# The first tiles of a decoder trunk's input projection in another order, and the norm's weight row spread with 128 rows of weights

## The reference

```
def rms_norm(x, g):
    xf = x.astype(jnp.float32)
    y = xf * lax.rsqrt(jnp.mean(xf * xf, axis=-1, keepdims=True) + EPS)
    return (y * g.astype(jnp.float32)).astype(x.dtype)

def trunk_layer(x, p, k_past, v_past, ...):
    h = rms_norm(x, g_pre_mix)
    cb, cc, ch, q, k, v, ga, gb = jnp.split(h @ w_in, IN_SPLITS, axis=-1)
    ...   # gated short convolution, stick-breaking attention, projections
    x = x + rms_norm(merged @ w_o, g_post_mix)
    ...   # up-projection, convolution, gelu gate, down-projection, input embedding
```

## Time and profile before

| | |
|---|---|
| median of three runs | 1679.24 us (1679.14 to 1679.53) |
| the profiled execution | 1680.04 us |
| its span, first to last instruction | 1678.3 us |
| TensorE busy | 1667.5 us, 99% of the span |
| VectorE, ScalarE, GpSimd busy | 1101.4, 794.6, 321.0 us |
| moved by transfers | 170.64 MB, 102 GB/s in the mean |

### The profile page before, as it was taken

The page is one execution under the profiler, slowest core; times in us unless marked ns, Lnnn a source line. Parts: engine busy times, 40 slices in busy tenths (PEclk is TensorE's granted clock), DMA queues, the critical chain, the costliest instruction groups (busy, mean ns, idle before and its releaser), DMA issues.

```text
span 1678.3 us, 27174 instructions
## 1 busy us (share of the span) xinstructions
PE 1667.5 (99%) x9101; PEld 1462.9 (87%) x9101; DVE 1101.4 (66%) x1606; ACT 794.6 (47%) x1391; POOL 321.0 (19%) x268
## 2 busy tenths in 40 slices
PE   9999999999999999999999999999999999999998
PEld 8999998999999999988888888888888878888886
DVE  7365246325533646547688888888888688776576
ACT  7345344444534453125454444444444444465675
POOL 2000000000000000002346666666664000000000
PEclk9999999999999999999999999999999999999999
DMA  5312221132123114443132222222222852245333
GB/s 182 97 55 74 80 77 55 57 99 68 60 67 92 53 63 149 151 169 116 68 97 80 79 79 79 79 72 72 79 79 97 293 191 80 90 150 186 112 123 118
DMA packets 176598, 170.64 MB, mean 102 GB/s; under 512 B 16207, under 2 KB 144555, under 8 KB 176492
## 3 DMA queue, kind: packets, MB, share of 16 engines
q1 hardware_dynamic: 165546, 164.41, 30.5%
q10 hardware_dynamic: 10946, 4.91, 1.0%
HBM read 129.66 MB, written 39.62 MB: 101 GB/s over the span
## 4 chain that ended last, share of the span: by engine, by line
PE 94%; DVE 3%; DMA 1%; issue 1%; SPq 1%; ACT 0%; DVEq 0%; POOL 0%; POOLq 0%; ACTq 0%
PE pair L3152 11%; PE pair L2840 9%; PE pair L2842 9%; PE pair L2841 9%; PE pair L3212 8%; PE pair L3214 8%; PE pair L3213 8%; PE pair L2794 6%; PE pair L3368 3%; PE pair L3370 3%; PE pair L3369 3%; PE pair L3221 3%; PE pair L3021 2%; PE pair L2771 2%; PE pair L2769 2%; PE pair L2770 2%
## 5 line engine op out<-in xcount | busy, mean ns | idle before, releaser
L2840 PE MATMUL pair<-xh,wh 128*128 128x384 f32 (+1 forms) x952 | 324.4, 341 | 0.0
L2842 PE MATMUL pair<-xh,wl 128*128 128x384 f32 (+1 forms) x952 | 311.3, 327 | 0.0
L2841 PE MATMUL pair<-xl,wh 128*128 128x384 f32 (+1 forms) x952 | 310.8, 326 | 0.0
L2840 PEld LDWEIGHTS pair<-xh,wh 128*128 128x128 f32 x952 | 179.3, 188 | 5.4 <-issue 4.0
L2841 PEld LDWEIGHTS pair<-xl,wh 128*128 128x128 f32 x952 | 179.4, 188 | 0.0
L2842 PEld LDWEIGHTS pair<-xh,wl 128*128 128x128 f32 x952 | 178.8, 188 | 0.0
L1074 POOL TENSOR_TENSOR srow<-hn,hn 128x512 f32<-128x512 f32 x8 | 12.0, 1506 | 791.1 <-DVE hn L2322 790.8
L3368 PE MATMUL pair<-woph,foph 128*128 128x512 f32 x308 | 120.9, 393 | 0.1
L3370 PE MATMUL pair<-woph,fopl 128*128 128x512 f32 x308 | 120.0, 390 | 0.0
L3369 PE MATMUL pair<-wopl,foph 128*128 128x512 f32 x308 | 120.0, 390 | 0.0
L1408 ACT ACTIVATE keep<-pair,bias 128x512 f32<-128x512 f32 (+4 forms) x100 | 58.2, 582 | 115.6 <-DVE pair L2175 71.5
(11 more groups left out here) (417 smaller groups left out, 4289.5 us busy)
## 6 DMA issues: line engine op xcount, KB each, us to landing
rawp<-in_w_up SPq DMA_DIRECT2D x88, 256.0 KB, 3.8
raw<-in_w_in SPq DMA_DIRECT2D x80, 256.0 KB, 3.2
wd<-in_w_down SPq DMA_DIRECT2D x55, 256.0 KB, 3.0
f_spill<-cv SPq DMA_DIRECT2D x22, 552.0 KB, 2.8
f<-f_spill SPq DMA_DIRECT2D x44, 256.0 KB, 5.6
gat<-gate_spill SPq DMA_DIRECT2D x16, 544.0 KB, 4.5
x_spill<-x SPq DMA_DIRECT2D x16, 512.0 KB, 3.0
gate_spill<-stg SPq DMA_DIRECT2D x32, 192.0 KB, 1.9
```

What stands on the lines that cost most here:

```text
L2840: t_.matmul(b, h, xhi, start=(k == 0), stop=False, skip_group_check=True)
L2841: t_.matmul(b, h, xlo, start=False, stop=False, skip_group_check=True)
L2842: ins = t_.matmul(b, l, xhi, start=False, stop=(k == KD - 1), skip_group_check=True)
```

## The change

It has five parts.

- `grow` becomes 128 rows of which row 0 is the weight row that counts: `ones` is 128 x 128 with ones in row 0 and zeros elsewhere. Rows 0 to 31 of `grow` are loaded (a broadcast of the same row, 128 KB), rows 32 to 63 are zeroed by GpSimd, rows 64 to 127 by VectorE. The result is the same row on all partitions.
- The fillers go from 34 to 14: six before the row products, eight behind them.
- The products of the first tiles are reordered: block 0's high products come first, before its low part and the low weights are waited for, turn 2 comes earlier among them, and in the other two units the products with the part that comes latest stand last.
- ScalarE makes block 0's high part ahead of block 2's square.
- The low weights of job 1 are made by VectorE in place of GpSimd.

```diff
-WARM = (8, 4, 11, 5, 6)
+WARM = (8, 6)
...
-        grow, ones = a.take("grow", [1, D]), a.take("ones", [1, P])
+        grow, ones = a.take("grow", [P, D]), a.take("ones", [P, P])
...
+            pool.wait_ge(g_const, 1)
+            g.memset(grow[32:64, :], 0.0).then_inc(g_grow, 1)
+            pool.wait_ge(g_grow, 1)
             then(g.memset(far[:, :], 0.0))
...
-            for j in range(2):
-                pool.wait_ge(a_hi, j + 1)
-                minus(wl[j][:, :], raw[j][:, :], f(wh[j][:, :])).then_inc(g_wlo, 1)
+            pool.wait_ge(a_hi, 1)
+            minus(wl[0][:, :], raw[0][:, :], f(wh[0][:, :])).then_inc(g_wlo, 1)
...
-            act.dma_start(grow[:, :], inp["g_pre_mix"]).then_inc(row_in, 16)
+            act.dma_start(grow[0:32, :], inp["g_pre_mix"].rearrange("l d -> (l d)").partition_broadcast(32)).then_inc(row_in, 16)
...
             whi()
+            x0_high(0)
             x0_square(2)
-            x0_high(0)
...
-            v.memset(ones[:, :], 1.0).then_inc(d_ones, 1)
+            then(v.memset(ones[:, :], 0.0))
+            v.memset(ones[0:1, :], 1.0).then_inc(d_ones, 1)
+            v.memset(grow[64:P, :], 0.0).then_inc(d_ones, 1)
...
                     x0_scaled(3, 1, 4)
-                    wlo_by_pool()
+                    wlo()
...
                 def by_blocks():
                     b = open_unit(0, 0)
...
+                    o, cols = b[:, 0:P], slice(0, P)
+                    pe.wait_ge(a_hi, 1)
+                    pe.wait_ge(a_x0h, 2)
+                    for k in range(KD):
+                        t_.matmul(o, tall(0, k)[0], xh[:, k, cols], ...)
+                    begin_job()
+                    pe.wait_ge(d_x0l, 2)
+                    for k in range(KD):
+                        if k == 3:
+                            x0_turn(2)
+                        h, l = tall(0, k)
+                        t_.matmul(o, h, xl[:, k, cols], ...)
+                        t_.matmul(o, l, xh[:, k, cols], ...)
+                    o, cols = b[:, P:3 * P], slice(P, 3 * P)
+                    for k in range(KD):
+                        if k % KH == 0:
+                            pe.wait_ge(a_x0h, 5 + k // KH)
+                        h, l = tall(0, k)
+                        t_.matmul(o, h, xh[:, k, cols], ...)
+                        t_.matmul(o, l, xh[:, k, cols], ...)
+                    pe.wait_ge(d_x0l, 6)
+                    for k in range(KD):
+                        ins = t_.matmul(o, tall(0, k)[0], xl[:, k, cols], ...)
+                    ins.then_inc(p_unit, 1)
...
                 if first:
-                    idle(4)
-                    pe.wait_ge(d_ones, 1)
+                    idle(1)
+                    pe.wait_ge(d_ones, 2)
+                    pe.wait_ge(g_grow, 1)
                     pe.wait_ge(row_in, 16)
...
                     idle(0)
                     x0_turn(0)
-                    idle(1)
                     x0_turn(1)
-                    idle(2)
-                    begin_job()
                     by_blocks()
-                    begin_job()
-                    in_tile(1, 0, {1: [(x0_turn, 3)], 3: [(x0_turn, 4)], 5: [(x0_turn, 5)]})
-                    pe.wait_ge(d_x0l, 12)
-                    conv_rows()
-                    in_tile(0, 1, {6: [(x0_turn, 6)]})
+                    weight_low_last(1, 0, {1: 3, 7: 4, KD + 1: 5})
+                    block_low_last(0, 1, {6: 6})
                     past(0)
```

More of the change, by code:

```diff
@@ L520, in build @@
         a_sum, d_sum = sem("a_sum"), sem("g_wlo_d_sum")
-        g_wlo, SUM0 = d_sum, 2
+        g_grow, SUM0 = d_sum, 2
+        g_wlo, WLO0 = d_sum, 1
         d_lo = sem("d_lo")
@@ L1977, in wlo_by_pool @@
             def wlo_by_pool():
-                dve.wait_ge(g_wlo, job.step())
+                dve.wait_ge(g_wlo, WLO0 + job.step())
                 dve.sem_inc(d_lo, 1)
@@ L2854, in idle @@
                     for _ in range(WARM[i]):
-                        turned(banks[1 if i in (2, 3) else 7][:, 0:P], ident[:, :])
+                        turned(banks[7][:, 0:P], ident[:, :])
                 def by_blocks():
                     b = open_unit(0, 0)
[L2860 to L2871, removed]
+                    o, cols = b[:, 0:P], slice(0, P)
@@ new lines, in by_blocks @@
+                    pe.wait_ge(a_hi, 1)
+                    pe.wait_ge(a_x0h, 2)
+                    for k in range(KD):
+                        t_.matmul(o, tall(0, k)[0], xh[:, k, cols], start=(k == 0), stop=False, skip_group_check=True)
+                    begin_job()
[4 more added lines that the diff above has]
+                        h, l = tall(0, k)
+                        t_.matmul(o, h, xl[:, k, cols], start=False, stop=False, skip_group_check=True)
+                        t_.matmul(o, l, xh[:, k, cols], start=False, stop=(k == KD - 1), skip_group_check=True)
@@ new lines, in by_blocks @@
+                    o, cols = b[:, P:3 * P], slice(P, 3 * P)
[3 more added lines that the diff above has]
+                        h, l = tall(0, k)
+                        t_.matmul(o, h, xh[:, k, cols], start=(k == 0), stop=False, skip_group_check=True)
+                        t_.matmul(o, l, xh[:, k, cols], start=False, stop=False, skip_group_check=True)
+                    pe.wait_ge(d_x0l, 6)
@@ new lines, in by_blocks, with weight_low_last @@
+                    for k in range(KD):
+                        ins = t_.matmul(o, tall(0, k)[0], xl[:, k, cols], start=False, stop=(k == KD - 1), skip_group_check=True)
+                    ins.then_inc(p_unit, 1)
+                def weight_low_last(j, gr, between):
+                    b = open_unit(j, gr)
+                    xhi, xlo = (lambda k: part(xh[:, k, :], gr)), (lambda k: part(xl[:, k, :], gr))
+                    pe.wait_ge(a_hi, j + 1)
+                    for k in range(KD):
+                        if k in between:
+                            x0_turn(between[k])
+                        h = tall(j, k)[0]
+                        t_.matmul(b, h, xhi(k), start=(k == 0), stop=False, skip_group_check=True)
+                        t_.matmul(b, h, xlo(k), start=False, stop=False, skip_group_check=True)
+                    begin_job()
+                    for k in range(KD):
+                        if KD + k in between:
+                            x0_turn(between[KD + k])
+                        ins = t_.matmul(b, tall(j, k)[1], xhi(k), start=False, stop=(k == KD - 1), skip_group_check=True)
+                    ins.then_inc(p_unit, 1)
@@ new lines, in block_low_last @@
+                def block_low_last(j, gr, between):
+                    b = open_unit(j, gr)
+                    xhi, xlo = (lambda k: part(xh[:, k, :], gr)), (lambda k: part(xl[:, k, :], gr))
+                    for k in range(KD):
+                        if k % KH == 0:
+                            pe.wait_ge(a_x0h, 6 * gr + 5 + k // KH)
+                        h, l = tall(j, k)
+                        t_.matmul(b, h, xhi(k), start=(k == 0), stop=False, skip_group_check=True)
+                        t_.matmul(b, l, xhi(k), start=False, stop=False, skip_group_check=True)
+                    pe.wait_ge(d_x0l, 6 * gr + 6)
+                    conv_rows()
+                    for k in range(KD):
+                        if k in between:
+                            x0_turn(between[k])
+                        ins = t_.matmul(b, tall(j, k)[0], xlo(k), start=False, stop=(k == KD - 1), skip_group_check=True)
```

## The result

The changed kernel takes 1682.68 us in the median of 20 runs (1679.12 to 1685.34), the kernel before 1679.47 (1678.73 to 1680.31, 20 runs). The ratio is 1.0017 with a 95% interval of 1.0011 to 1.0022: the medians differ by 3.2 us, upwards, where 2.3 us less was forecast; the time lies outside the stated range. The spread is new as well: 6 us in place of 1.6. The mean granted clock of each run goes with its time: the two fastest runs (1679.12 and 1679.76) have 0.999, like the profiled execution of before, the other eighteen 0.998 to 0.995.

What follows compares the result with a forecast made beforehand. TensorE, busy 1667.5 of 1678.3 us, was taken as the bound. The first tile's 1.3 us (0.60 + 0.23 + 0.50) plus 1.0 us of waits made 2.3, giving a median of 1676.9 us; range 1676.0 to 1679.0.

Steps and rivals of the forecast that it cites:

- row's load: Start of the kernel: the 128 KB row lands so that TensorE's row products start at 3.5 us.
- removing them gains nothing by itself: Fillers before turn 1 and the first unit: they only filled waits, so their removal was put at no gain.
- R2: Rival, 13%: row lands past 3.9, VectorE's block 1 Newton step waits behind GpSimd till 11.75; gain 0.35, 1678.9 us.
- R3: Rival, 4%: without fillers TensorE's clock stays at the lower level through the first tile; 3.9 us slower, 1683.1 us.
- R4: Rival, 7%: x not delayed by the row's bytes, gain 2.6; a better high part or transition might give 3.3, 1676.0.
- 0.3 us for each x block: First x loads: the row's further 124 KB through busy DMA engines at 397 GB/s make each block 0.3 us later.
- 3.78 us for the products, rows or not: TensorE's row products at the start: with 128 rows they keep 3.78 us at the lower clock level.
- The clock up before turn 0: TensorE before 8.84 us: the clock has risen by then, since full-array work begins at 1.60 and not 6.78.
- Fillers, 0.5 us: Five fillers between block 0's products and those of blocks 1 and 2: removing them gains 5 x 0.1 = 0.5 us.
- High part first: Block 0's high part ahead of block 2's square: it starts at 9.5, turn 2 stands at 14.44; gain 0.60 us.
- Order of the first tiles: Ten products instead of twelve behind turn 2 gain 0.23 us; the first tile ends 1.3 us sooner, other gains included.
- Low weights of job 1 on VectorE, 1.0 us: VectorE makes them, its 2.05 us stall goes, and TensorE's waits of 0.7 and 0.3 us vanish: 1.0 us.

Runs made afterwards that it cites:

- e1: The changed kernel with the one-row products and 4 KB load of before, no fills; 14 fillers, new order and VectorE's low weights stay: 1678.78 us, ratio 0.9993.
- e11: The kernel before with 14 fillers in place of 34, the twenty behind turn 0 gone, nothing else: 1678.83 us, ratio 0.9995.
- e5: The kernel of e1 with 4 fillers put ahead of turn 1 and 12 ahead of turn 2: 1677.85 us, ratio 0.9990.
- e8: The changed kernel, 128-row row included, with 22 fillers ahead of turn 1 and 12 ahead of turn 2: 1679.94 us, ratio 1.0004.
- e4: The kernel before with only the row spread by 128 rows (128 KB load, both fills); 34 fillers and old order: 1682.11 us, ratio 1.0013.
- e2: The changed kernel with GpSimd's low weights of job 0 held until block 1 is scaled: 1679.36 us, ratio 1.0005.
- e9: The kernel of e5 with a 128 KB broadcast of the row behind the 4 KB one, unused until block 2 is scaled: 1677.84 us, ratio 0.9991.
- e3: The changed kernel with the four fillers before turn 1 and the eleven before the first unit put back: 1681.04 us, ratio 1.0009.
- e7: The kernel of e5 with block 2's square ahead of block 0's high part again, as before the change: 1677.81 us, ratio 0.9992.
- e6: The kernel before with one edit, job 1's low weights by VectorE in place of GpSimd: 1678.51 us, ratio 0.9994.
- e10: The kernel of e8 with GpSimd's low weights of job 0 held until block 1 is scaled: 1680.70 us, ratio 1.0004.

## Why the prediction was wrong, step by step

**Which step failed.** Two. The first is the term of the row's load: the products were to start at 3.5 us and started at 4.90. The second is "removing them gains nothing by itself": the fillers' hold on the clock was put at nothing, and without them, where the late row or the new order leaves TensorE waiting, the clock fell: in 18 of 20 runs of the changed kernel, for 6.8 us in the trace, and in 6 of 11 of e1. In e11, where only the fillers are gone and the longest wait is 0.8 us, one run of eleven has the lower mean. On top of it R2 and R3 were treated as apart. R2's mechanism came as written (row past 3.9, step behind GpSimd's product); what R2 left out is that its own 2 us of waiting, with the fillers gone, lets the clock fall. That combination is the usual run, and I gave R3 4% because I priced it as three waits of 1 us. R2's size was not far off for runs without the fall: it said 1678.9, the two undisturbed runs of the changed kernel took 1679.12 and 1679.76. R3's 1683.1 lies close to the measured 1682.68 by luck: it had the lower level stay from the start, and here the clock rose near 10.2, fell at 13.8 and came back at 20.7.

**The sum in measured terms.** From e5 (1677.85) the changed kernel differs by the row (e8 less e5: 2.1 us) and by the clock (changed kernel less e8: 2.7 us); that the two add up to 1682.68 is so by the way they are taken. Other pairs give like sizes. The row: e4 less before 2.5, and the undisturbed runs of e2 less those of e1, 1.7 without the collision. The clock: the median of the changed kernel lies 2.9 and 3.6 us above its own two undisturbed runs, and half of 6.8 us at the lower level are 3.4.

- *Row's load, 3.5 us.* It was 4.90, and 4.54 to 5.06 in the six traces with the 128-row product. My interpolation by bytes between 3.07 and 4.63 took the load as free of the x blocks it shares the engines with. It was used 0.6 us ahead of the first x block (5.49): three quarters of the way from 3.07 to there, not one.
- *0.3 us for each x block.* 0.94 in e9, 0.86 in the changed kernel. The rate of 397 GB/s was read at 10 to 12.5 us; the changed kernel's transfers moved 33, 115, 324 and 340 GB/s in the four microseconds from 1 to 5 (57, 180, 348 and 413 before), so bytes over 397 was the wrong quotient.
- *3.78 us for the products, rows or not.* 3.75 us with 128 rows. Right; 3.37 in e3, where the clock rose during them.
- *Fills and GpSimd's other fills.* Ready at 2.55, its last fill ended at 9.2. Right, hidden.
- *The clock up before turn 0.* Half right. In the six traces with 128 rows TensorE is at the faster pace by 10.3 us at the latest, in e3 within the row products already; in the seven with one row between 10.0 and 12.9. In the changed kernel it came near 10.2, not before 8.84. So this part of the change brings the rise forward by about 2 us, though its products start 1.5 to 2 us later; whether the rows or the wait ahead of them do it, no run separates. What comes behind waits for data, so it gains nothing.
- *Fillers, 0.5 us.* Right in size (e11: 0.7 with everything they stood in the way of). Wrong as to the rest: removing them can lose 3.5 us a run where another edit leaves a wait.
- *High part first.* 0.60 us for turn 2 was forecast together with the fillers' going; the swap by itself gains nothing (e7).
- *Order of the first tiles.* e7 less e6 is the order with the fillers moved: 0.7 us in the medians, 1.0 at the page turn. Forecast 1.3 with the fillers.
- *Low weights of job 1 on VectorE, 1.0 us.* 0.8 (e6).
- *The sum without the row, 2.3 us.* In e1's five undisturbed runs 2.3 us; in e5 2.4 us at the page turn, 1.4 in the median.
- *"Comes off the end one for one."* Not in these traces: of 2.4 us at the page turn 1.8 are left in the span (e5), of 2.3 us lost 2.0 (changed kernel).
- *"Faster 7%."* It doesn't follow from the prediction's own numbers: R4's largest gain, 3.3 us, is below the 3.4 us from which it counts a change.

**What the pages said.** The two-input step of 1.73 us starts behind GpSimd's product and ends with it (12.18), as the 2.21 us one did. The Trainium skill, page "SBUF — State Buffer", section "Who interferes with whom", says that a VectorE instruction with two SBUF inputs contends with a GpSimd instruction that reads SBUF; the traces of the changed kernel, e3, e4 and e8 agree, and e2 and e10 remove it by order alone. The Trainium skill, page "TensorE: Matmul & The Clock Gate", section "Part 4: PE-mode transpose", says that transposes don't count as busy in the same way, and that the full clock doesn't come from them. e5 and e8 speak against it as the trace of before did: with turns of the identity alone in those waits the clock stayed up in 22 of 22 runs, where it fell in 18 of 20 (changed kernel) and 6 of 11 (e1) without them; e1 ran on another chip than those two, and the changed kernel's isn't known.

**What stays open.** Why e5's gain is 2.4 us at the page turn and 1.4 in the median is known in part. In e5's trace TensorE waits 0.7 and 0.6 us for low weights of the last stage, where before has one such wait of 0.7: 2.4 less 0.6 are the 1.8 us between the two spans. What causes the second wait, and the 0.4 us from there to the medians, isn't known. Nor is it known why e1's undisturbed runs gain 2.3 us and e5 1.4: the fillers and the chip differ. Whether e5's fillers would hold the clock on the chip of e1 wasn't run; e9 and e10 (22 runs on a third chip) had no fall either. Whether the 128-row product would pay with a load that lands in time wasn't tried: its rows 1 to 31 have to be cleared or loaded first.

## What to carry to other kernels

Fillers on TensorE are not idle weight: in these kernels a wait left bare near the start could drop the clock, and the drop (1.5 to 3.5 us here) outweighs what the fillers cost (0.7). Put them exactly where the trace shows TensorE waiting, and count the wait again after every other edit: fillers sized for a wait that is gone are themselves the wait (e10), and then hide what the edit gained. A load of 128 KB issued beside the first x blocks was used at 4.5 to 5.1 us and put the first block off by 0.8 us, where 4 KB were there by 3.1, so a broadcast that grows at the very start is priced by what it delays, not by its bytes. And where two rivals share a cause, one's wait may be the other's condition: price the chain, not each by itself.

## What the runs showed of the hardware

- The clock fell after a stillness of 2.2 us (changed kernel, at 13.8 us), of 1.3 us (e1, at 14.8 us) and of 2.2 us (e3, at 14.7 us), each time 0.1 to 1.1 us after TensorE was at work again, and stayed at 0.50 for 6.8, 3.4 and 3.4 us with TensorE busy. But length alone doesn't decide: in e4, where the fillers of before stand on either side, a wait of 1.9 us was passed, and none of its 11 runs has the lower mean.
- The granted clock in the trace shows such a fall (0.50) but reads 1.00 in the first 12 us, while turns took 0.22 us and not 0.11; the first rise can be had from the pace alone.
- It varies by run: the same kernel has a lower mean clock in 5 of 11, 6 of 11 or 18 of 20 runs. A median of 3 runs would have shown e1 at anything from 1677.2 to 1680.9.
- A VectorE step of one column with two SBUF inputs took 1.72 to 2.05 us in place of 0.16 while GpSimd's product ran (changed kernel, e3, e4, e8), and ended with it; issued ahead of it, it took 0.16 (e2, e10).
